# High and low matmuls of a wide piece in turn

## The reference

```
first block:  x -> rms_norm -> @ w_in -> two attention groups -> @ w_out -> + x
              -> rms_norm -> peer: q = x @ w_q; top experts by sub keys;
                 a = x . u[expert] ; w = gate * gelu(a) ; y = sum w * v[expert]
second block: rms_norm -> @ w_in -> two attentions, gated branches -> @ w_out
              -> rms_norm -> u = relu(h @ w_up)^2 -> u @ w_down
```

## Time and profile before

| | us |
|---|---|
| median of 3 runs | 3250.3 |
| lowest, highest | 3248.05, 3251.49 |
| profiled execution | 3252.63 |
| its span, first to last instruction | 3250.8 |
| PE matmul busy in the span | 3198.1 |
| DVE, ACT, POOL busy | 2096.5, 1517.3, 522.7 |

### The profile page before, as it was taken

One profiled execution on the slowest core, in us unless ns is written; L12 is line 12 of the kernel. 1 busy time (PEld: TensorE's weight loads), 2 busy tenths in 40 slices (PEclk: granted clock), 3 DMA queues, 4 the chain that ended last, 5 costly groups with the idle time before them and its releaser, 6 DMA issues.

```text
span 3250.8 us, 41898 instructions
## 1 busy us (share of the span) xinstructions
PE 3198.1 (98%) x16112; PEld 2716.0 (84%) x16112; DVE 2096.5 (64%) x3062; ACT 1517.3 (47%) x2006; POOL 522.7 (16%) x322
## 2 busy tenths in 40 slices
PE   8899999999999999999999999999999999999998
PEld 7788888888888878888888888888888888888886
DVE  6766588887555576666666565565465655555556
ACT  5645454454444444444444444455444544444443
POOL 0010005777777700000000000000000000000000
PEclk9999999999999999999999999999999999999999
DMA  6457557888888877776666655455555556666664
GB/s 218 150 183 252 181 180 210 215 210 216 214 213 209 217 284 246 249 247 245 241 231 203 203 187 175 162 173 184 189 191 191 180 189 193 188 194 190 190 192 148
DMA packets 220296, 661.03 MB, mean 203 GB/s; under 512 B 56705, under 2 KB 56849, under 8 KB 217537
## 3 DMA queue, kind: packets, MB, share of 16 engines
q1 hardware_dynamic: 170864, 600.81, 56.5%
q0 software_dynamic: 49232, 57.54, 8.6%
HBM read 622.48 MB, written 35.78 MB: 202 GB/s over the span
## 4 chain that ended last, share of the span: by engine, by line
PE 74%; POOL 14%; issue 4%; DVE 4%; DMA 3%; ACT 1%; DVEq 0%; ACTq 0%; SPq 0%; POOLq 0%
PE PS L1650 72%; POOL scr_g L2710 14%; DMA scr_g<-M 2%; PE PS L1728 2%; DVE wlo L2113 1%; ACT whi L1881 1%; DMA M<-scr_g 0%; DVE R L2617 0%; DVE AA L2159 0%; ACT M L1923 0%; DVE M L2518 0%; DMA TMP<-in_key_pos 0%; DMA R<-in_x 0%; ACT Y L1967 0%; DVE BB L2159 0%
## 5 line engine op out<-in xcount | busy, mean ns | idle before, releaser
L2113 DVE TENSOR_TENSOR wlo<-raw,whi 128x1024 fp32r<-128x1024 f32 x1101 | 1339.9, 1223 | 742.5 <-ACT whi L1881 735.8
L1881 ACT ACTIVATE whi<-raw 128x1024 fp32r<-128x1024 f32 x1101 | 1153.6, 1056 | 863.7 <-PE PS L1650 810.8
L1650 PE MATMUL PS<-whi,AA 128*128 128x512 f32 (+1 forms) x2880 | 719.7, 390 | 5.2 <-ACT whi L1881 3.5
L1650 PE MATMUL PS<-whi,BB 128*128 128x512 f32 x2640 | 666.6, 393 | 1.7 <-DVE wlo L2113 1.2
L1650 PEld LDWEIGHTS PS<-whi,AA 128*128 128x128 f32 x2880 | 537.2, 189 | 117.0 <-DVE AA L2525 3.1
L1650 PE MATMUL PS<-BB,whi 128*128 128x512 f32 x2304 | 577.3, 392 | 1.7 <-DVE BB L2159 1.7
L1650 PEld LDWEIGHTS PS<-whi,BB 128*128 128x128 f32 x2640 | 491.2, 188 | 102.2 <-DVE wlo L2113 1.6
L2710 POOL DMA_INDIRECT scr_g<-M x256 | 477.6, 1866 | 379.2 <-DVE M L2490 238.1
L1650 PEld LDWEIGHTS PS<-BB,whi 128*128 128x128 f32 x2304 | 414.4, 189 | 76.0 <-DVE BB L2159 1.9
L1650 PE MATMUL PS<-wlo,AA 128*128 128x512 f32 (+1 forms) x1440 | 389.1, 387 | 0.0
L1650 PE MATMUL PS<-wlo,BB 128*128 128x512 f32 x1320 | 356.4, 389 | 0.5 <-DVE wlo L2113 0.5
(11 more groups left out here) (236 smaller groups left out, 1486.9 us busy)
## 6 DMA issues: line engine op xcount, KB each, us to landing
raw<-in_peer_u SPq DMA_DIRECT2D x256, 512.0 KB
raw<-in_peer_v SPq DMA_DIRECT2D x256, 512.0 KB
raw<-in_w_in SPq DMA_DIRECT2D x160, 512.0 KB
raw<-in_w_up SPq DMA_DIRECT2D x128, 512.0 KB
raw<-in_w_down SPq DMA_DIRECT2D x128, 512.0 KB
raw<-in_w_out SPq DMA_DIRECT2D x64, 512.0 KB
raw<-in_w_in_a SPq DMA_DIRECT2D x32, 512.0 KB
scr_g<-M POOLq DMA_DIRECT2D x8, 2048.0 KB, 32.0
```

The costliest lines, as they stand in the source:

```text
L1650: return e.matmul(outp, l, r, start=start, stop=stop)
L1881: e.activation(whi[:, n % NH, :], raw[:, n % NR, :], ACT.Copy).then_inc(s_hi, 1)
L2113: e.tensor_tensor(wlo[:, n % NH, :], raw[:, n % NR, :], bf(whi[:, n % NH, :]), ALU.subtract).then_inc(s_lo, 1)
```

## The change

`wide_piece` now goes through nine steps. In step n it issues the high matmul of block n (if n is below 8) and then the low matmul of block n-1 (if n is 1 or more; `LAG` is 1). So the order is H0, H1, L0, H2, L1, ... H7, L6, L7. The wait for the low split stands behind H0 and ahead of H1; `piece_hi_used` is raised by H7, which has six low matmuls ahead of it, and `piece_used` by L7. The matmuls, their operands, banks and first and last marks are the same.

```diff
@@ -46,7 +46,7 @@
     ALU, ACT, AX = mybir.AluOpType, mybir.ActivationFunctionType, mybir.AxisListType
 
     LEAD, LEADT = 3, 4
-    NR, NH, NST = 5, 3, 1080
+    NR, NH, NST, LAG = 5, 3, 1080, 1
 
     with ExitStack() as ctx:
         def sb(name, shape, dt=f32):
@@ -1705,20 +1705,21 @@
                     e.wait_ge(*mark)
                 for mark in high:
                     e.wait_ge(*mark)
-                for kk in range(4):
-                    kt = 4 * c + kk
-                    x = both[:, kt, :, :].rearrange("p a n -> p (a n)")
-                    for m in range(2):
-                        w = slice(256 * kk + 128 * m, 256 * kk + 128 * m + 128)
-                        last = mm(b[m][:, :], whi[:, s, w], x, kt == 0, False)
-                last.then_inc(s_hi_used, 1)
-                for mark in low:
-                    e.wait_ge(*mark)
-                for kk in range(4):
-                    kt = 4 * c + kk
-                    for m in range(2):
-                        w = slice(256 * kk + 128 * m, 256 * kk + 128 * m + 128)
-                        last = mm(b[m][:, 0:256], wlo[:, s, w], both[:, kt, 0, :], False, kt == 15)
+                for n in range(8 + LAG):
+                    if n == LAG:
+                        for mark in low:
+                            e.wait_ge(*mark)
+                    if n < 8:
+                        kk, m = n // 2, n % 2
+                        w = slice(128 * n, 128 * n + 128)
+                        x = both[:, 4 * c + kk, :, :].rearrange("p a n -> p (a n)")
+                        high_last = mm(b[m][:, :], whi[:, s, w], x, c == 0 and kk == 0, False)
+                        if n == 7:
+                            high_last.then_inc(s_hi_used, 1)
+                    if n >= LAG:
+                        kk, m = (n - LAG) // 2, (n - LAG) % 2
+                        w = slice(128 * (n - LAG), 128 * (n - LAG) + 128)
+                        last = mm(b[m][:, 0:256], wlo[:, s, w], both[:, 4 * c + kk, 0, :], False, c == 3 and kk == 3)
                 last.then_inc(s_used, 1)
 
             def transpose(srcs, bank, ready):
```

## The result

The kernel after takes 3264.28 us (median of 5 runs, 3263.15 to 3265.22) against 3250.3 before: a ratio of 1.0042 (1.0031 to 1.0053). It is slower by 14 us, where I forecast 5 us faster.

The account below looks back on a forecast made before the run. PE's matmul cadence in wide pieces was taken as the bound; -8.1 (cadence) + 0.3 (late release) + 2.4 (gate fetch) = -5.4 us, from 3252.6 to 3247, given as 3245 because the median is 2.3 lower; range 3230 to 3266.

Parts of the forecast that it names:

- What bounds the kernel: Expert products' wide pieces: PE's own matmul cadence sets the time, 2.793 us a piece over 416 pieces, 1162 us.
- The cadence: Wide pieces: a high and a low matmul cost 346.7 ns together, 0.0194 us a piece less, -8.1 us over 416.
- The toll: PE's matmuls: a weight load of 128 columns takes 13.3 ns from the stream beside it, whatever its length.
- the disturbance is renewed at each change of length: Rival, wide pieces: pairs stay at 348 to 351 ns, 0 to +6 us, 3253 us; chance 0.25.
- slower: Rival, wide pieces: each low matmul costs 120 ns and each high 235, pair 355, +19.6 us, 3270 us; chance 0.18.
- Loads hidden: Rival, wide pieces: weight loads hide entirely, pair 340 ns, -30.4 us on the cadence, -15.7 in all, 3235 us; chance 0.17.
- Banks: Wide pieces: L0 and H2 writing the same bank in succession, 256 columns apart, costs nothing.
- The late release and early wait: Wide pieces: high buffer released six low matmuls later (0.69 us), low split waited for before H1; +0.3 us.
- the cover: Wide pieces: the low split ends ahead of its new wait point; 2.1 us of that lead stay after the late release.
- The gate fetch: Behind POOL's scatters: its landing does not move with PE, so DVE waits longer; 2.4 us of gain given back.

Follow-up runs that it names:

- the half loads: Kernel before, but `w_up`'s high matmuls behind the first two of each unit load 64 weight columns, not 128; 3248.3 us in one execution, 3252.79 before beside it.
- the order of two and two: Kernel before with wide-piece matmuls reordered to two high, two low in turn (H H L L ...); 3251.09 us, ratio 0.9998.
- the strict alternation: The change with `LAG` 0 instead of 1, so wide pieces run H0 L0 H1 L1 ... H7 L7; 3254.98 us, ratio 1.0022 to the kernel before.
- the late release and early wait alone: Kernel before, its order kept, with the high buffer released six low matmuls late and the low split waited for behind H0; 3252.26 us, ratio 1.0002.
- the beginnings: Kernel before with units of wide pieces reordered: 31 different starts of low and high matmuls behind whole runs, then strict alternation; 3252.06 us in one execution.

## Why the prediction was wrong

*What bounds the kernel* was right: the cadence of PE in wide pieces sets the time, no wait does; PE's waits did not grow.

The number, 3264.3, lies inside the range of 3230 to 3266, but that is luck: none of the cases that the range was drawn for came about.

*The cadence* was wrong, and it is the step "I take 346.7: it is the price of each load counted once, and I expect what a low one saves by coming first to be paid by the next high one". That exchange is real, to the nanosecond: in the short cadence the high one takes 230.0 and the low one 116.7, against 226.7 and 120 in runs. But the alternation has a second cadence, of 353 ns, and which one runs is settled by the matmuls ahead. I treated the pair as one price with an uncertainty; it has two values, and a piece of H H ... L L holds the upper. Measured: 352.5 in the change's piece, +11.1 us, for -8.1 forecast.

*The toll* of 13.3 ns for 128 loaded columns, on which that price stood, fell with the half loads. Two equations had been solved for two unknowns and one more row agreed (113.6 for 113.4); that row streams 256 columns throughout and says nothing of a load beside 512.

*The rivals.* The number lies between two of them: "the disturbance is renewed at each change of length" (348 to 351) and "slower" (355), past the point of 351.1 from which I had the slower one decide. In mechanism the first is nearer: the highs stay at what the first ones behind a low run cost (235.0) and the lows keep part of their saving (117.5 for 116). But it isn't renewed by each change, as the order of two and two (2.7867 a piece) and the short cadence show. The slower rival's reason, that a load for a high one now lies under 256 columns, holds in the short cadence too, where a high one costs 230.

*Loads hidden* (340): in no run. The Trainium skill (TensorE: Matmul & The Clock Gate, part 2, "What happens when you issue a matmul") says that loading the next weights takes no read bandwidth from the running matmul. No run here measures read bandwidth. The half loads do not contradict the sentence, since they freed nothing in the matmuls whose loads were halved (1.85 us for eight, with 1.84). The hidden load that I drew from it does not follow from it, and loads do bear on the spacing: halving them unsettled it.

*Banks*: right. In the strict alternation a high and its low write one bank in succession, and 346.7 is all that a pair takes; with the change's own order of banks the piece at 340 us has 347.

*The late release and early wait*: put at 0.3 us; measured at none that shows (1.0002, with an interval of 3 us either way, so 0.3 is not told from nothing), with ACT's waits doubled and the cover holding.

*The gate fetch*, +2.4: void. I took its time in the profile before for its time after; the scatters took 1866 ns each before and 1733 after, and the fetch left 45 us sooner, so there was nothing to run into. What sped the scatters up stays open: the half loads, with the expert products of before, have 1883, and the late release and early wait alone 1738.

So -5.4 became +11.1 on the cadence, and 12.2 with the waits and clock of the first `w_up` stretch; the narrow pieces and the rest gave back 1.7, which makes the 10.5 of the spans.

**What stays open.** Why two cadences exist: which part of TensorE the load and the stream meet in. The half loads show that the loads bear on it, and the beginnings that no other engine decides; more was not tried. Nor do I know why strict alternation fell into the short cadence in the expert products of one execution. There the first high one, behind matmuls of 128 columns, took 284 ns; at 405.69 us, behind such matmuls too, it took 287, and that stretch was long.

## What to carry to other kernels

Where matmuls of different length follow one another back to back, their spacing can have more than one steady value for the same order, and what was issued before decides which; read the starts over whole stretches, and test an order on the chip with the edges that it will have. A price fitted to two rows is a fit: change the quantity that it names (here the loaded columns) before building on it. And a time at which another engine happened to finish in the profile before is no fixed point in the kernel after: here it moved by 45 us.

## What the runs showed of the hardware

- A pair of 512 and 256 columns has two steady cadences at the 2.4 GHz level, 346.7 and 353.3 ns, and where PE does not wait the same beginning leads to the same one each time (31 beginnings, twice each, alike to 1 ns).
- Loading 64 columns instead of 128 does not shorten the spacing of 512-column matmuls in runs of eight: mean 230.7 ns, where with 128 they average 230.1 and settle at 226.7.
- At a granted clock of 0.50, the 1.2 GHz level, there is none of this: three pairs from 2533.52 to 2535.44 take 1.92 us, 640 ns each, 427 + 213, two to one as the columns are. Half of 640 would be 320; the short cadence is 27 ns above that, the long one 33.
